# Two transformer layers on one core: the four norms worked in two parts of the tokens

## The chip, the cores and the metric

The kernel runs on one core of a Trainium2 chip. The metric is the device time of one execution in microseconds (us). TensorE (PE) multiplies, VectorE (DVE), ScalarE (ACT) and GpSimd (POOL) do the rest, SyncE (SP) issues the transfers.

## What is computed

```python
for i in range(DEPTH):                       # 2 layers, 1024 features
    sh1, sc1, g1, sh2, sc2, g2 = ada_modulation(c, ada_w[i], ada_b[i])
    a_lat = h * (1 + sc1) + sh1              # the same for 256 context tokens
    y = attn_mixer(...) if i % 2 == 0 else gla_mixer(...)
    h = layer_norm(DEEPNORM_ALPHA * h + g1 * y, ln_g[i, 0], ln_b[i, 0])
    f = conv_ffn(h * (1 + sc2) + sh2, ffn_w_up[i], ...)
    h = layer_norm(DEEPNORM_ALPHA * h + g2 * f, ln_g[i, 1], ln_b[i, 1])
```

The first layer works on 512 latent and 256 context tokens, 768 in all; behind its second norm the context is needed by the GLA mixer's states, and from there on only the 512 latent tokens have a residual stream. So there are four layer norms: norm 0 behind the attention projection and norm 1 behind the first FFN, over 768 tokens, norm 2 behind the GLA output and norm 3 behind the last FFN, over 512.

## The kernel before, in words

Features lie on the partitions, tokens in the free dimension. `h_res` holds the residual stream as 8 tiles (KT) of 128 features by 768 tokens. A weight matrix is cut into slabs: one slab is the weights of one output tile, 128 by 1024. There are 185 of them, in one fixed order over the whole kernel, read by SyncE into four `raw` buffers. ScalarE rounds a slab to fp32r (`w_hi`, L940), VectorE takes the rest (`w_lo`, L1358), both in two buffers. Activations are split alike into `x_hi` and `x_lo`. A slab is then 3 products per input tile: w_hi x_hi, w_hi x_lo, w_lo x_hi (`slab`, L464), each over 512 tokens and, where the context is in, over 256 more. FFN down slabs of the last group have 6 input tiles instead of 8.

Each engine runs its own hand-written list, and semaphores tie them. Around a norm the lists say:

- TensorE: the last eight slabs (numbers 0 to 7), then `stats`: products of `mean_w` with the sum of tiles 0 to 6 (L541), then with tile 7 and its square (L548), then two products per 128 tokens that spread mean and inverse root over the partitions (L531). Then `first_modulated`: the first two slabs of the next matrix together, tile by tile as x_hi and x_lo come (L505, L510); the second of them leaves out the last 2 tiles (3 over 512 tokens) until the first is done.
- ScalarE, per slab: w_hi of the slab after next, the gated copy out of PSUM (`tmp`, L1060, L1062), the square (`sq_t`, L1070). Then the root (L1087) and per tile `mod_t` (L959) and `x_hi` (L970).
- VectorE, per slab: w_lo, the residual (L1563), the running sum (L1570). In norm 0 it also makes modulation values of the next stages (L1382, L1384) behind slabs 1, 3 and 5, and `fuse` behind slab 6. Then five small operations (L1615 to L1626), the reciprocal (L1629), and over each tile of `h_res` two passes: less the mean (L1634), times the inverse root (L1640), both read from PSUM. x_lo of tiles 0, 3, 6 (L1646).
- GpSimd: the running sum of the squares (L1940), x_lo of the other five tiles (L1922).
- In norm 3 there is no modulation: ScalarE applies gain and bias (L1091) and SyncE writes each of the 8 tiles out (L445).

Everything runs over all tokens of the norm at once.

## Time and profile before

| | |
|---|---|
| median of 3 runs | 1747.23 us (1746.46 to 1747.8) |
| the profiled execution's own time | 1749.78 us |
| its span | 1748.0 us |
| mean granted TensorE clock | 0.985 |
| TensorE busy | 1671.9 us, 96% |
| TensorE weight loads | 1398.0 us, 80% |
| VectorE busy | 1122.3 us, 64% |
| ScalarE busy | 713.5 us, 41% |
| GpSimd busy | 85.9 us, 5% |

Busy time of TensorE counts matmuls with modelled ends, and they overlap: a mean matmul lasts longer than the distance to the next. The distance from start to start is what one costs in a stream. The granted clock is in shares of 2.4 GHz.

### The profile page before, as it was taken

Reading aid. Unit: us, or ns where it says so; the run is one execution under the profiler, and the core shown is the slowest. Engines: PE = TensorE matmul, PEld = TensorE weight load, DVE = VectorE, ACT = ScalarE, POOL = GpSimd, SP = SyncE. Lnnn points to the kernel's source line nnn. Section 1 sums busy time; section 2 is a strip of 40 time slices with the busy share of each in tenths; the row PEclk is TensorE's granted clock in tenths of the full one; section 3 lists DMA queues with packets and bytes.
Section 4 is the critical chain, followed back from the end, with each engine's and each line's share of the span. In section 5 each row is a group of like instructions: output and inputs, shape, how many; then the busy total and the mean of one; then the engine's idle time right before and its main releaser. Section 6 shows DMA issues by size and latency. Waiting matters only on the chain.

```text
span 1748.0 us, 23892 instructions
## 1 busy us (share of the span) xinstructions
PE 1671.9 (96%) x9008; PEld 1398.0 (80%) x9008; DVE 1122.3 (64%) x1816; ACT 713.5 (41%) x1060; POOL 85.9 (5%) x57
## 2 busy tenths in 40 slices
PE   7999999998999999999999899989989899999997
PEld 6888877887888888888888787857677688888885
DVE  6678666477787577864865554187755664464456
ACT  4212565335333223322334663256544543343345
POOL 0200000122000000000002200000002100000002
PEclk9999999999999999999999999999989999999998
DMA  8344100031433334333322112011112233333332
GB/s 355 110 149 157 49 1 1 25 133 39 143 122 121 130 108 144 104 136 133 109 62 85 49 49 61 24 35 37 37 49 84 62 96 95 96 96 97 96 96 73
DMA packets 37280, 159.51 MB, mean 91 GB/s; under 512 B 4145, under 2 KB 4401, under 8 KB 31057
## 3 DMA queue, kind: packets, MB, share of 16 engines
q1 hardware_dynamic: 37202, 158.44, 27.4%
q8 instruction: 52, 0.85, 0.2%
q14 instruction: 26, 0.21, 0.0%
HBM read 156.33 MB, written 2.10 MB: 91 GB/s over the span
## 4 chain that ended last, share of the span: by engine, by line
PE 87%; DVE 5%; ACT 4%; issue 2%; DMA 1%; SPq 0%; POOL 0%; ACTq 0%; DVEq 0%
PE pm L464 65%; PE pm L698 4%; PE pm L874 3%; PE pm L618 2%; PE pm L484 2%; PE pm L644 2%; PE pm L817 2%; PE pm L631 1%; ACT mod_t L959 1%; DMA ada_w<-first_ada 1%; PE pm L799 1%; DVE h_res L1634 1%; PE pm L575 1%; ACT w_hi L940 1%; PE pm L531 1%
## 5 line engine op out<-in xcount | busy, mean ns | idle before, releaser
L1358 DVE TENSOR_TENSOR w_lo<-raw,w_hi 128x1024 fp32r<-128x1024 f32 x185 | 230.4, 1247 | 374.2 <-ACT w_hi L940 371.7
L940 ACT ACTIVATE w_hi<-raw 128x1024 fp32r<-128x1024 f32 x181 | 191.8, 1060 | 638.3 <-PE pm L464 576.1
L464 PE MATMUL pm<-x_hi,w_hi 128*128 128x512 f32 (+1 forms) x1536 | 446.1, 352 | 3.6 <-DVE w_lo L1358 3.6
L464 PE MATMUL pm<-x_hi,w_lo 128*128 128x512 f32 (+1 forms) x1536 | 448.7, 354 | 0.0
L464 PE MATMUL pm<-x_lo,w_hi 128*128 128x512 f32 (+1 forms) x1536 | 444.1, 351 | 0.0
L464 PEld LDWEIGHTS pm<-x_hi,w_hi 128*128 128x128 f32 x1536 | 250.2, 189 | 49.4 <-DVE w_lo L1358 6.0
L464 PEld LDWEIGHTS pm<-x_hi,w_lo 128*128 128x128 f32 x1536 | 248.8, 189 | 39.6
L464 PEld LDWEIGHTS pm<-x_lo,w_hi 128*128 128x128 f32 x1536 | 247.2, 188 | 41.4
L464 PE MATMUL pm<-hid_hi,w_hi 128*128 128x512 f32 (+1 forms) x396 | 119.5, 356 | 1.7 <-DVE w_lo L1358 1.7
L464 PE MATMUL pm<-hid_hi,w_lo 128*128 128x512 f32 (+1 forms) x396 | 120.7, 359 | 0.0
L464 PE MATMUL pm<-hid_lo,w_hi 128*128 128x512 f32 (+1 forms) x396 | 119.3, 355 | 0.0
L1384 DVE CUSTOM_DVE_ANT_0 ada_w<-ada_w,cond_rep 128x1024 f32<-128x1024 f32 x80 | 102.5, 1281 | 0.0
L1940 POOL TENSOR_TENSOR sum<-sum,sq_t 128x768 f32<-128x768 f32 (+1 forms) x28 | 46.9, 1674 | 953.0 <-ACT sq_t L1070 953.0
L1126 ACT ACTIVATE hid_hi<-hid_f 128x768 f32 (+3 forms) x44 | 32.6, 741 | 124.6 <-DVE hid_f L1695 124.6
L464 PEld LDWEIGHTS pm<-hid_hi,w_hi 128*128 128x128 f32 x396 | 65.7, 189 | 14.9 <-DVE w_lo L1358 3.0
L464 PEld LDWEIGHTS pm<-hid_hi,w_lo 128*128 128x128 f32 x396 | 65.3, 188 | 10.8
L464 PEld LDWEIGHTS pm<-hid_lo,w_hi 128*128 128x128 f32 x396 | 64.7, 188 | 11.2
L874 PE MATMUL pm<-x_sum,raw 128*128 128x512 f32 x128 | 60.8, 610 | 8.4 <-issue 8.4
L1382 DVE CUSTOM_DVE_ANT_0 junk_f<-ada_w,cond_rep 128x1024 f32<-128x1024 f32 x56 | 68.3, 1219 | 0.0
L1698 DVE TENSOR_TENSOR hid_lo<-hid_f,hid_hi 128x512 f32 (+2 forms) x44 | 36.3, 825 | 44.7 <-ACT hid_hi L1126 44.7
L618 PE MATMUL pm<-qkv 128*128 128x256 f32 (+3 forms) x176 | 55.3, 419 | 2.1 <-ACT probs_t L1006 1.3
L644 PE MATMUL pm<-probs_t,v_tok 128*128 128x128 f32 x400 | 53.9, 279 | 1.5 <-DVE x_lo L1493 0.7
(224 smaller groups left out, 2363.2 us busy)
## 6 DMA issues: line engine op xcount, KB each, us to landing
raw<-slabs SPq DMA_DIRECT2D x185, 512.0 KB, 3.6
ada_w<-ada SPq DMA_DIRECT2D x44, 1024.0 KB, 4.9
ada_w<-first_ada SPq DMA_DIRECT2D x4, 1024.0 KB, 19.1
raw<-gates SPq DMA_DIRECT2D x8, 512.0 KB, 3.6
h_res<-x SPq DMA_DIRECT2D x4, 768.0 KB, 17.1
out<-h_res SPq DMA_DIRECT2D x8, 256.0 KB, 2.0
rope<-rope SPq DMA_DIRECT2D x1, 512.0 KB, 23.9
level_f<-level SPq DMA_DIRECT2D x1, 448.0 KB, 3.3
```

The source lines that it names most:

```text
L464: last = pe.matmul(out_p[:, a:b], w[slot][:, ks], x[:, k, a:b], start=(k == 0 and w is w_hi and x is hi), stop=(k == tiles - 1 and w is w_lo))
L484: last = pe.matmul(pm[slot][:, a:b], w[slot][:, ks], x[:, k, a:b], start=(n == 0 and w is w_hi and x is hi), stop=(n == KT - 1 and w is w_lo))
L618: last = pe.matmul(pm[n % 3][:, at:at + b - a], q, qkv[:, u["k"], a:b], start=True, stop=(u["band"] is None or at > 0))
L644: last = pe.matmul(weighed(n), v_tok[:, t, u["v"] * P:(u["v"] + 1) * P], probs_t[:, n % 2, j * P:(j + 1) * P], start=(j == 0), stop=(j == ...
L698: last = pe.matmul(pm[j][:, a:b], w[slot][:, ks], x[:, k, a:b], start=(k == 0 and w is w_hi and x is hid_hi), stop=(k == tiles - 1 and w i ...
L874: last = pe.matmul(gate_bank, gate_raw(i)[:, k * P:(k + 1) * P], x_sum[k][:, :], start=(k == 0), stop=(k == KT - 1))
L940: act.activation(w_hi[nxt % 2][:, :], raw[nxt % 4][:, :], ACT.Copy).then_inc(sem["split_hi"], 1)
L1358: dve.tensor_tensor(w_lo[nxt % 2][:, :], raw[nxt % 4][:, :], w_hi[nxt % 2][:, :].bitcast(FP32), ALU.subtract).then_inc(sem["split_lo"], 1)
L1382: junk_written = order.mark(dve.tensor_tensor_reduce(junk[:, :], w, cond_rep[:, 0, :], 1.0, 0.0, ALU.mult, ALU.add, to[:, half, 0:1]))
L1384: last = dve.tensor_tensor_reduce(w, w, cond_rep[:, 1, :], 1.0, 0.0, ALU.mult, ALU.add, to[:, half, 1:2])
L1698: dve.tensor_tensor(hid_lo[:, bass.ds(2 * i + u // 2, 1), 0:tokens].rearrange("p a b -> p (a b)"), hid_f[:, 0:tokens], hid_hi[:, bass.ds(2 ...
L1940: pool.tensor_tensor(sum2[:, 0:tokens], sum2[:, 0:tokens], sq_t[:, n % 2, 0:tokens], ALU.add).then_inc(sem["summed"], 1)
```

## The change

A norm is worked in two parts of its tokens (`norm_halves`): 0 to 511 and 512 to 767 where it has 768, 0 to 255 and 256 to 511 where it has 512. `h` is the part, `TAIL` is slab 6.

- TensorE's `tail` runs slab 6 and slab 7 over the first part, then the first part's sums (`first_sums`), slab 6 over the second part, the sums with tile 7 (`last_sums`), half of slab 7 over the second part, the spreading of the first part's statistics, the rest of slab 7, and the second part's sums. `first_modulated` goes through 16 places, the 8 tiles of the first part and then the 8 of the second; the second slab runs two places behind the first, and the second part's statistics are spread behind place 4. The third slab (`slab_high_first`) does all products with w_hi before those with w_lo.
- ScalarE and VectorE take slabs 6 and 7 out of PSUM part by part (`take`, `squares`, `half`), find mean and root part by part (`variance`, `root`, `inverse`), and interleave the second part's with the normalising of the first. All passes over `h_res`, `mod_t`, `x_hi`, `x_lo` are one part wide. Both slabs' splits for the next matrix now stand inside the tail and the first part.
- GpSimd's last sum and its x_lo are one part wide. SyncE writes 16 pieces instead of 8.
- In norm 0 VectorE's modulation values stand behind slabs 1, 2 and 4, `fuse` behind slab 5.

The diff, cut to its core:

```diff
-RESIDUALS = (KT, 4 * KT, 5 * KT, 8 * KT)
+RESIDUALS = (0, 3 * KT + 2, 4 * KT + 4, 7 * KT + 6)
+TAIL = KT - 2
+PER_NORM = KT + 2
...
+        def norm_halves(tokens):
+
+            return ((0, LAT), (LAT, TOK)) if tokens == TOK else ((0, CTX), (CTX, LAT))
...
+            def slab_high_first(base, u, hi, lo, tokens, banks):
...
+                for w, xs in ((w_hi, (hi, lo)), (w_lo, (hi,))):
+                    if w is w_lo:
+                        pe.wait_ge(sem["split_lo"], s + 1)
+                    for k in range(KT):
+                        for x in xs:
+                            for a, b in halves:
+                                last = pe.matmul(out_p[:, a:b], w[slot][:, k * P:(k + 1) * P], x[:, k, a:b],
+                                                 start=(k == 0 and w is w_hi and x is hi),
+                                                 stop=(k == KT - 1 and w is w_lo))
+                last.then_inc(sem["slab_done"], 1)
...
-                one, two = base % 2, (base + 1) % 2
-                for k in range(KT):
-                    slots = (one, two) if k < KT - lag else (one,)
-                    pe.wait_ge(sem["x_hi_done"], KT * (c + 1) + k + 1)
-                    for slot in slots:
-                        high(slot, k)
-                    pe.wait_ge(*low_of(c, k))
-                    for slot in slots:
-                        last = low(slot, k)
-                last.then_inc(sem["slab_done"], 1)
-                for k in range(KT - lag, KT):
-                    high(two, k)
-                    last = low(two, k)
-                last.then_inc(sem["slab_done"], 1)
...
+                def visit(j, i):
+                    if tokens == LAT and i == KT:
+                        low(j, *places[i - 1])
+                    if i < len(places):
+                        high(j, *places[i])
+                    if i >= 1 and not (tokens == LAT and i == KT):
+                        low(j, *places[i - 1])
+                behind = 2
+                pe.wait_ge(sem["split_lo"], base + 1)
+                for i in range(len(places) + behind + 1):
+                    if i < len(places):
+                        h, k = places[i]
+                        pe.wait_ge(sem["x_hi_done"], modded(c, h, k))
+                    if i <= len(places):
+                        visit(0, i)
+                    if i == behind:
+                        pe.wait_ge(sem["split_lo"], base + 2)
+                    if i >= behind:
+                        visit(1, i - behind)
+                    if i == 4:
+                        spread_stats(c, 1, tokens)
...
+                half_slab(TAIL, 0)
+                half_slab(TAIL + 1, 0)
+                first_sums(c, 0, tokens)
+                half_slab(TAIL, 1)
+                last_sums(c, 0, tokens)
+                half_slab(TAIL + 1, 1, 0, tiles // 2)
+                spread_stats(c, 0, tokens)
+                half_slab(TAIL + 1, 1, tiles // 2)
+                first_sums(c, 1, tokens)
+                last_sums(c, 1, tokens)
...
+                    take(TAIL, 0)
+                    squares(TAIL, 0)
+                    take(TAIL + 1, 0)
+                    squares(TAIL + 1, 0)
+                    take(TAIL, 1)
+                    if norm < 3:
+                        split(base + KT, base + KT)
+                    root(norm, 0, tokens)
+                    squares(TAIL, 1)
...
+                take, squares = last_half
+                for h, (a, b) in enumerate(norm_halves(tokens)):
                     for n in range(KT):
-                        act.wait_ge(sem["centred"], KT * c + n + 1)
-                        act.activation(h_res[:, n, 0:tokens], h_res[:, n, 0:tokens], ACT.Identity, bias=col("ln_b", KT * c + n),
-                                       scale=col("ln_g", KT * c + n)).then_inc(sem["h_ready"], 1)
-                    return
-                for n in range(KT):
-                    act.wait_ge(sem["centred"], KT * c + n + 1)
-                    modulate(n, c, tokens)
-
-            residual_phase(S_ATTN_OUT, 0, G1, TOK, norm=0)
-            norm_phase(0, TOK)
+                        act.wait_ge(sem["centred"], normed_at(c, h, n))
+                        if c < 3:
+                            modulate(n, c, h, tokens)
+                        else:
+                            act.activation(h_res[:, n, a:b], h_res[:, n, a:b], ACT.Identity, bias=col("ln_b", KT * c + n),
+                                           scale=col("ln_g", KT * c + n)).then_inc(sem["h_ready"], 1)
+                        if h == 0 and n == 0:
+                            take(KT - 1, 1)
+                            if c < 3:
+                                split(after_base + 1, after_base + 1)
+                            squares(KT - 1, 1)
+                        if h == 0 and n == 2:
+                            root(c, 1, tokens)
...
-                            if j in (1, 3, 5):
+                            if j in (1, 2, 4):
...
+                    half(TAIL, 0)
+                    half(TAIL + 1, 0)
+                    variance(norm, 0, tokens)
+                    half(TAIL, 1)
+                    inverse(norm, 0, tokens)
+                    if norm < 3:
+                        rest(base + KT, base + KT)
...
+                    dve.wait_ge(sem["spread"], 4 * c + 2 * h + 1)
+                    less_mean(0)
+                    dve.wait_ge(sem["spread"], 4 * c + 2 * h + 2)
+                    scaled(0)
+                    if h == 0:
+                        last_half(KT - 1, 1)
+                    for n in range(1, KT + 3 if c < 3 else KT + 1):
+                        if n < KT:
+                            less_mean(n)
+                        if 2 <= n <= KT:
+                            scaled(n - 1)
+                        if h == 0 and n == 2 and c < 3:
+                            rest(after_base + 1, after_base + 1)
+                        if h == 0 and n == 4:
+                            variance(c, 1, tokens)
+                        if h == 0 and n == 6:
+                            inverse(c, 1, tokens)
...
+            for h, (a, b) in enumerate(norm_halves(LAT)):
+                for n in range(KT):
+                    sp.wait_ge(sem["h_ready"], KT * h + n + 1)
+                    sp.dma_start(out[:, n, a:b], h_res[:, n, a:b]).then_inc(sem["out_done"], 16)
...
+                for h, (a, b) in enumerate(norm_halves(tokens)):
+                    pool.wait_ge(sem["squared_h"], PER_NORM * c + TAIL + 1 + 2 * h)
+                    pool.wait_ge(sem["summed"], KT * c + TAIL + h)
+                    pool.tensor_tensor(sum2[:, a:b], sum2[:, a:b], sq_t[:, TAIL % 2, a:b], ALU.add).then_inc(sem["summed"], 1)
```

The order of VectorE's instructions in norm 0, before, from the last residual on. L1563 is the residual of slab 7, L1358 w_lo of the next slab, L1634 the subtraction of the mean, L1640 the scaling:

```order
L1607 TENSOR_TENSOR fused<-fused,mods 128x16
L1563 SCALAR_TENSOR_TENSOR h_res<-h_res,tmp 128x768
L1358 TENSOR_TENSOR w_lo_61<-raw_55,w_hi_59 128x1024
L1615 COPY stat_a<-pm 128x12
L1619 TENSOR_TENSOR small<-pm,stat_a 128x6
L1621 TENSOR_TENSOR small<-small 128x6
L1623 TENSOR_TENSOR small<-stat_a,small 128x6
L1626 TENSOR_TENSOR small<-pm,small 128x6
L1629 RECIPROCAL small<-small 128x6
L1634 TENSOR_TENSOR h_res<-h_res,pm 128x768 x3
L1640 TENSOR_TENSOR h_res<-h_res,pm 128x768
L1634 TENSOR_TENSOR h_res<-h_res,pm 128x768
```

And in the change, from the residual half of slab 6 over the second part (L1720) to the first part's third tile. L1790 is the reciprocal, L1488 w_lo, L1797 the subtraction, L1802 the scaling:

```order
L1720 SCALAR_TENSOR_TENSOR h_res<-h_res,tmp 128x256
L1726 TENSOR_TENSOR sum_96<-sum_96,h_res 128x256
L1790 RECIPROCAL small<-small 128x4
L1488 TENSOR_TENSOR w_lo_60<-raw_54,w_hi_58 128x1024
L1797 TENSOR_TENSOR h_res<-h_res,pm 128x512
L1802 TENSOR_TENSOR h_res<-h_res,pm 128x512
L1720 SCALAR_TENSOR_TENSOR h_res<-h_res,tmp 128x256
L1797 TENSOR_TENSOR h_res<-h_res,pm 128x512 x2
L1802 TENSOR_TENSOR h_res<-h_res,pm 128x512
L1488 TENSOR_TENSOR w_lo_61<-raw_55,w_hi_59 128x1024
L1797 TENSOR_TENSOR h_res<-h_res,pm 128x512
L1802 TENSOR_TENSOR h_res<-h_res,pm 128x512
```

The last residual half and two splits now stand between reciprocal and third tile, and the passes are 512 wide in the first part.

ScalarE's in norm 0, before, around the root (L1087):

```order
L1060 ACTIVATE tmp<-pm,mods 128x512
L1060 ACTIVATE tmp<-pm,mods 128x256
L1070 ACTIVATE sq_t<-h_res 128x768
L940 ACTIVATE w_hi_59<-raw_55 128x1024
L1087 ACT_TABLE_LOAD
L1087 ACTIVATE small<-small,vec 128x6
L959 ACTIVATE x_hi<-h_res,fused 128x512
L959 ACTIVATE x_hi<-h_res,fused 128x256
L959 ACTIVATE mod_t<-h_res,fused 128x512
L959 ACTIVATE mod_t<-h_res,fused 128x256
L959 ACTIVATE mod_t<-h_res,fused 128x512
```

And in the change. L1175 is the copy out of PSUM, L1014 the split of a slab, L1186 the square, L1209 the root, L1046 the modulation, L1056 x_hi:

```order
L1175 ACTIVATE tmp<-pm,mods 128x256
L1014 ACTIVATE w_hi_58<-raw_54 128x1024
L1209 ACT_TABLE_LOAD
L1209 ACTIVATE small<-small,vec 128x4
L1186 ACTIVATE sq_t<-h_res 128x256
L1046 ACTIVATE x_hi<-h_res,fused 128x512
L1046 ACTIVATE mod_t<-h_res,fused 128x512
L1175 ACTIVATE tmp<-pm,mods 128x256
L1014 ACTIVATE w_hi_59<-raw_55 128x1024
L1186 ACTIVATE sq_t<-h_res 128x256
L1046 ACTIVATE mod_t<-h_res,fused 128x512
L1056 ACTIVATE x_hi<-mod_t 128x512
```

A copy, a split and a square stand between the modulations of tile 0 and tile 1. The rows that follow there, tile 2, the second part's root and tile 3:

```order
L1046 ACTIVATE mod_t<-h_res,fused 128x512
L1056 ACTIVATE x_hi<-mod_t 128x512
L1209 ACTIVATE small<-small,vec 128x2
L1046 ACTIVATE mod_t<-h_res,fused 128x512
L1056 ACTIVATE x_hi<-mod_t 128x512
```

Tile 3's modulation is behind the root in the list.

## Rows read from the trace of the kernel before

**Rows 1.** The page, part 1: busy us, share, instructions.
```profile
PE 1671.9 (96%) x9008; PEld 1398.0 (80%) x9008; DVE 1122.3 (64%) x1816; ACT 713.5 (41%) x1060; POOL 85.9 (5%) x57
```

**Rows 2.** Windows of A to D: span, busy by engine (records), PE clock, DMA share, GB/s.
```profile
387.06:421.73 34.67, 28.66 (x170) 23.78 (x169) 21.18 (x29) 23.66 (x34) 9.87 (x6) 0.95 0.05 16
964.57:998.79 34.22, 28.74 (x170) 24.04 (x168) 21.58 (x30) 23.22 (x33) 9.21 (x5) 0.95 0.05 16
1352.20:1377.85 25.65, 20.15 (x97) 15.22 (x97) 15.88 (x29) 15.81 (x23) 6.89 (x6) 0.93 0.07 24
1730.16:1748.00 17.84, 5.76 (x49) 5.40 (x48) 11.34 (x23) 9.18 (x12) 0.00 (x0) 0.73 0.31 118
```

**Rows 3.** Timeline in A: start us, us, engine, line, operation, [idle before].
```profile
387.06 2.84 PE L541 MATMUL pm<-mean_w,sum 128*128 128x128 f32 x24
...
391.27 1.28 ACT L1087 ACT_TABLE_LOAD   x1
...
394.49 2.68 DVE L1634 TENSOR_TENSOR h_res<-h_res,pm 128x768 f32<-128x768 f32 x3 [0.54 <-PE pm L531]
...
398.07 1.30 ACT L959 ACTIVATE x_hi<-h_res,fused 128x512 fp32r<-128x512 f32 x2 [4.35 <-DVE h_res L1640]
...
419.36 1.06 ACT L940 ACTIVATE w_hi<-raw 128x1024 fp32r<-128x1024 f32 x1 [2.59 <-PE pm L510]
```

**Rows 4.** Timeline, TensorE's products: in A over 768 tokens, in C over 512.
```profile
386.35 0.51 PE L464 MATMUL pm<-x_lo,w_hi 128*128 128x512 f32 x2
386.70 0.53 PE L464 MATMUL pm<-x_hi,w_lo 128*128 128x512 f32 x2
...
1351.78 0.39 PE L464 MATMUL pm<-o_lo,w_hi 128*128 128x512 f32 x1
1352.01 0.39 PE L464 MATMUL pm<-o_hi,w_lo 128*128 128x512 f32 x1
```

**Rows 5.** Timeline of ScalarE in A and C; last, a group by line and form.
```profile
405.50 1.29 ACT L959 ACTIVATE mod_t<-h_res,fused 128x512 f32<-128x512 f32 x2
...
407.57 1.30 ACT L959 ACTIVATE mod_t<-h_res,fused 128x512 f32<-128x512 f32 x2
...
1370.70 0.80 ACT L959 ACTIVATE mod_t<-h_res,fused 128x512 f32<-128x512 f32 x1
...
1371.53 0.63 ACT L970 ACTIVATE x_hi<-mod_t 128x512 fp32r<-128x512 f32 x1
...
1372.07 0.80 ACT L959 ACTIVATE mod_t<-h_res,fused 128x512 f32<-128x512 f32 x1
...
L959 ACT ACTIVATE mod_t<-h_res,fused 128x256 f32<-128x256 f32 x16 | 9.4, 586 | 0.0
```

**Rows 6.** Timeline in D: VectorE's last passes and ScalarE's last step.
```profile
1742.01 0.68 DVE L1634 TENSOR_TENSOR h_res<-h_res,pm 128x512 f32<-128x512 f32 x1
...
1742.60 1.87 DVE L1640 TENSOR_TENSOR h_res<-h_res,pm 128x512 f32<-128x512 f32 x3
1743.32 2.22 ACT L1091 ACTIVATE h_res<-h_res,vec 128x512 f32<-128x512 f32 x3 [0.38 <-DVE h_res L1640]
```

**Rows 7.** Timeline of VectorE in the GLA heads: passes of 256 columns.
```profile
1153.15 0.42 DVE L1773 TENSOR_TENSOR sides<-cum 128x256 f32<-128x256 f32 x1
1153.48 0.42 DVE L1774 TENSOR_TENSOR sides<-cum 128x256 f32<-128x256 f32 x1
```

**Rows 8.** Timeline of GpSimd: x_lo over 768 tokens and over 512.
```profile
412.69 1.84 POOL L1922 TENSOR_TENSOR x_lo<-mod_t,x_hi 128x768 fp32r<-128x768 f32 x1 [1.01 <-ACT x_hi L970]
...
1368.81 1.29 POOL L1922 TENSOR_TENSOR x_lo<-mod_t,x_hi 128x512 fp32r<-128x512 f32 x1 [1.45 <-ACT x_hi L970]
```

**Rows 9.** Windows of low clock in A and C; timeline, TensorE's first product in C.
```profile
400.70:404.00 3.30, 3.21 (x11) 2.42 (x10) 3.30 (x4) 2.51 (x4) 1.28 (x1) 0.52 0.00 0
...
1364.20:1366.60 2.40, 2.40 (x7) 1.83 (x7) 2.40 (x5) 2.07 (x3) 1.55 (x2) 0.53 0.00 0
...
1361.92 0.47 PE L505 MATMUL pm<-x_hi,w_hi 128*128 128x512 f32 x1 [2.38 <-ACT x_hi L959]
```

330 lines of the change are left out of this document (200 added, 130 removed).

## The prediction

> **What bounds the kernel now.** I read the page first: TensorE is busy 1671.9 of 1748.0 us [rows 1], so what a change can win lies where TensorE stands still or does small work, or behind its last product. The stretches around the four norms, taken next, hold this [rows 2]. A is the norm behind the attention projection (from the last product of its last slab to the first of the third FFN slab, 34.67 us), B the norm ahead of the GLA projections (to the first logits, 34.22 us), C the norm behind the GLA output (25.65 us), D the last norm (17.84 us, to the end of the span).
>
> How much of A is idle TensorE? A slab over 768 tokens has 24 pairs of a 512-wide and a 256-wide product, one pair each 0.352 us [rows 4], so 8.45 us, and the two slabs inside A are 16.9. The 36 statistics products are about 8.2 (12 of them take 2.84 with the tail of the last [rows 3]). So 9.6 us are idle in A, 9.1 in B. In C a slab over 512 tokens is 24 x 0.228 = 5.5 us [rows 4], two are 10.9, 24 statistics products 5.5: 9.2 idle. D has no slabs after it. 28 us is thus the most that A to C could give.
>
> What makes it wait is a chain of short steps: sums, root, spread, the subtraction of the mean at 394.49, x_hi of tile 0 from 398.07 [rows 3], and then one tile per ScalarE period, 2.07 us over 768 tokens (405.50 to 407.57) and 1.37 over 512 (1370.70 to 1372.07) [rows 5]. Two slabs want 2.11 and 1.37 us of TensorE per tile, so it is paced by ScalarE there. D is VectorE's: 16 passes over h_res, started 0.60 us apart (1742.01, 1742.60), then ScalarE's last step and the last transfer [rows 6].
>
> **Prices of the narrow pieces.** One 256-wide product is 0.352 - 0.228 = 0.125 us, so two halves cost 0.250 where one 512-wide product cost 0.228. Over 768 tokens the cut at 512 is where it was, and TensorE's work stays; over 512 tokens C has 4 slabs x 24 products x 0.022 = 2.1 us more, D 2 x 18 x 0.022 = 0.8. On VectorE 512 columns start 0.60 us apart [rows 6], 256 columns 0.335 (1153.15 to 1153.48) [rows 7]: 0.07 more for each pass cut in two. The 256-column rows read no PSUM, the norm's passes do; I take the same price. In the Trainium skill, "VectorE: DVE Perf Modes", section on the TRN2 errata, an fp32 tensor_tensor takes (N + 151) / 0.96 ns, which is 0.42 for 256, and small tiles pay the fixed part each. The durations here agree (0.42), the starts do not: half of the fixed part lies under the next pass. By the page the passes of D would take 32 x 0.42 - 16 x 0.69 = 2.4 us longer.
>
> By the rows they take 1.1 longer, and the sum goes by the rows. On ScalarE the modulation of 256 columns takes 0.586, the copy 0.42 (0.63 for 512 less half of what 1024 columns take more [rows 5, 3]), with a hand-off of 0.03 and 0.09 under the next: 0.94 a tile, over 512 columns 1.37. A tile of A or B therefore costs 2.31 where it cost 2.07, one of C 1.88 where it cost 1.37: 1.9 and 4.1 us more over eight tiles, on the engine that paces. GpSimd's 1.84 and 1.29 [rows 8] give 0.75 for 256 columns, within ScalarE's period.
>
> **Stage A, step by step**, on the clock of the profiled run. Slab 6 starts at 387.06 - 16.9 = 370.2. Its first part ends at 375.6, that of slab 7 at 381.1 (24 x 0.228 each). VectorE, which meets the last block of modulation products now behind slab 4 and not behind slab 5, comes out of its fuse near 377.4 by my list, so residual, square and GpSimd's sum of slab 6, first part, are there at 380.2: in time. first_sums to 382.9, slab 6 second part (24 x 0.125) to 385.9, last_sums to 387.7. ScalarE, behind take(6,1), the split of the next slab (1.06) and a table load of 1.28 [rows 3], has the root at 389.2; reciprocal 389.5, w_lo 390.7, and the first mean subtraction at 390.8, against 394.49: 3.7 us earlier. Scale at 391.5, x_hi of tile 0 out near 393.1 (was 399.4). Then four new things stand in the way. On ScalarE: mod, take(7,1), split (1.06), square, to 395.6. On VectorE: the residual half, then a w_lo between tiles 2 and 3. TensorE waits for the second part's last_sums until 396.1, then for tiles 1 and 2 (398.0, 400.4). And ScalarE's second Sqrt stands ahead of tile 3 (shown with the change) and waits for VectorE's variance, which comes only behind tiles 3 and 4: 400.4 to 402.0. So x_hi of tile 3 is ready at 403.4 (for all 768 tokens it was by 407.57 [rows 5]). From there TensorE has 14.6 us of products and 0.9 of spreads left and, with ScalarE at 1.37 a tile (it wants 1.37 itself), has no reason to stop: slab 0 done 418.1, slab 1 at 418.9. The third slab now needs only w_hi: 418.1 + 0.1 + 1.06 = 419.3, where it began at 421.73. **A: 2.4 us won**, if the clock holds. It does not now: in A the granted clock is 0.52 from 400.7 to 404.0 (the level of 1.2 GHz), in C 0.53 from 1364.2 to 1366.6, there behind an idle stretch of 2.38 us [rows 9]. After the change TensorE does some 2.3 us of products between 396 and 403.4, in bursts; I expect the same fall, from about 401.5, of which 2 us lie in dense work and cost 1.0. **A: 1.4 won.**
>
> **Stage B** has six tiles in slabs 6 and 7, so less work to lie under the statistics: slab 6 starts at 964.57 - 12.7 = 951.8, first parts end at 955.9 and 960.0, the root is ready at 967.4, w_lo at 968.9, first subtraction at 968.9. By the distances of A slab 0 ends at 968.9 + 27.3 = 996.2, slab 1 at 997.0. The logits wait for w_hi and then take_low on ScalarE, to 998.2 (was 998.79 [rows 2]): 0.5 won, less 1.0 for the clock. **B: 0.5 lost.**
>
> **Stage C.** Slab 6 starts at 1341.3; the narrow halves end at 1344.3 and 1347.3, GpSimd's sum lets first_sums go at 1347.6, the root is ready at 1353.5, VectorE starts at 1355.1. ScalarE then does 8 x 0.94 for each part with the square, split and Sqrt in between: x_hi of the last tile 1375.5, GpSimd's x_lo 1376.2, slab 0 done 1376.4, third slab 1377.6 (was 1377.85 [rows 2]). A low clock is hidden by ScalarE's pace. **C: 0.2 won**, call it nothing.
>
> **Stage D.** Slab 6 starts at 1722.0; TensorE waits 0.3 for w_lo, and 1.4 ahead of first_sums, because square, residual and GpSimd's 0.75 of slab 6 come behind those of slab 5. The root is ready at 1733.5, subtraction starts at 1734.1. From there VectorE has 32 passes x 0.335 = 10.7, the last residual half 0.45 and 1.2 of waiting for it (ScalarE takes slab 7's second part only at 1735.8), five small statistics and a reciprocal inside the first part, 1.2: its end is 1747.8, where it was 1744.5 [rows 6]. The narrow last ScalarE step and transfer give back 0.3. **D: 3.0 lost.** Output goes out in 16 transfers for 8; fifteen lie under the passes.
>
> Sum: -1.4 + 0.5 + 0 + 3.0 = +2.1 us. The profiled execution took 1749.78 for a span of 1748.0, the median of the runs is 1747.23; on the median the forecast is **1749.3 us**, on the profiled span 1750.1. Bounds by rows: A from 0.9 lost (low clock all through the first part) to 4 won (no wait for the second Sqrt), B 2.8 lost to 2.1 won, C 1.2 lost to 1.3 won, D 1 to 4 lost.
>
> **Rivals.** (1) *As worked out*, 0.38, with 1747 to 1752 of its own. (2) *The chain is shorter than I make it*: the variance of the second part does not hold ScalarE up (1.6 us), and TensorE's gaps stay short enough for 2.4 GHz. Then A 3.9, B 2.1, C 1.3 won, D 2.6 lost: 1742.5. For it: 28 us of idle are there, and the small steps overlap better in a real queue than in my list. Against it: the clock falls in A and C now, in C behind only 2.4 us. 0.27. (3) *No fall of the clock, all else as in 1*: 2.4 + 0.5 + 0.2 - 3.0 = 0.1 won, 1747.1. This is also where the change does not do what it says and only trades one wait for another. 0.15. (4) *Slower*: the bursts of two or three products between waits keep TensorE at 1.2 GHz well into the dense part. With twice the low stretch that A has now, 6.6 us at half speed in dense work cost 3.3 in A and B, and 1.4 in C: A 0.9, B 2.8, C 1.2, D 3.0 lost, 1755.1. It decides once more than 3 us of dense work run low. For it: the rows of the clock [rows 9], and TensorE is now the pacing engine from tile 3 on, so nothing hides it. Against: the quiet stretch is no longer than now. 0.20.
>
> The Trainium skill, "TensorE: Matmul & The Clock Gate", section on HAM oscillation, describes this: bursts with waits between them let the gate fall back each time. The fall behind 2.4 us of idle in C agrees.
>
> **Numbers.** 0.2%, 3.5 us, is about what a measurement can tell here: faster is below 1743.7, slower above 1750.7. Case 2 is faster in three of four; case 4 is slower nearly always, case 1 in one of four. That gives faster 0.24, same 0.46, slower 0.30. The range of 1742 to 1755 leaves out the ends of cases 2 and 4.
>
> **What would show it.** First subtraction of the mean 3 to 4 us nearer to slab 6's start in A, B and C; ScalarE idle ahead of the second Sqrt by 1 to 2 us; TensorE without waits from tile 3 on; a low granted clock between tile 1 and tile 5; D longer by 3 us with VectorE back to back at 0.335. I am wrong if a 256-wide product follows another at more than 0.13 us, if first_sums waits for GpSimd in A or B, or if D does not grow.

## The result, and the profile after

| | before | after |
|---|---|---|
| median of 6 runs each | 1746.65 us (1744.91 to 1747.8) | 1755.68 us (1753.95 to 1758.62) |
| the profiled execution's own time | 1749.78 us | 1758.62 us |
| its span | 1748.0 us | 1756.8 us |
| mean granted TensorE clock | 0.985 | 0.981 |

The ratio is 1.0053, 95% interval 1.004 to 1.0066: slower, clear of its interval, and just above the forecast's range. The page of after, part 1 (columns as in [rows 1]):

```profile
PE 1678.8 (96%) x9140; PEld 1409.5 (80%) x9140; DVE 1138.0 (65%) x1925; ACT 726.3 (41%) x1114; POOL 92.0 (5%) x76
```

Against [rows 1] every engine is busier, TensorE by 6.9 us, VectorE by 15.7, ScalarE by 12.8. To see where the span grew I cut both traces at the same places of the program: A from the attention output's first product to the third FFN slab, FFN 0 with its down slabs (504.30 us before, 504.31 after, not shown), B from just ahead of its last six down slabs to the logits, G from there to the GLA output's first product, C from that to the third slab of FFN 1, F to FFN 1's last six down slabs, D from those to the end. (These stretches are longer than the prediction's of the same letters, and each holds the same norm.) Windows of the kernel before (us of the window, TensorE's busy us and records, granted clock, DMA share, GB/s):

```profile
315.62:421.73 106.11, 98.61 (x573) 0.98 0.21 70
926.03:998.79 72.76, 67.28 (x388) 0.98 0.20 60
998.79:1299.20 300.41, 279.02 (x1473) 0.96 0.15 46
1299.20:1377.85 78.65, 68.97 (x315) 0.96 0.18 54
1377.85:1704.64 326.79, 324.60 (x1428) 1.00 0.32 97
1704.64:1748.00 43.36, 30.80 (x158) 0.89 0.21 73
```

The same windows of the kernel after:

```profile
314.92:418.58 103.66, 97.02 (x573) 0.98 0.21 72
922.89:997.42 74.53, 67.71 (x388) 0.95 0.19 59
997.42:1301.06 303.64, 282.20 (x1472) 0.95 0.14 45
1301.06:1382.24 81.18, 72.10 (x411) 0.94 0.17 52
1382.24:1708.66 326.42, 324.51 (x1428) 1.00 0.31 97
1708.66:1756.80 48.14, 34.53 (x194) 0.86 0.20 66
```

So A won 2.45 us, B lost 1.77, G 3.23, C 2.53, D 4.78; F and what lies ahead of A gave 0.4 and 0.7 (that first stretch, which no version touches, took 311.35 to 315.62 us in the fourteen traces behind this document, so its 0.7 is scatter). The sum is the 8.8 us between the spans. G is surprising: nothing in it but the order of one slab's products was changed. What differs is the clock's column. Stretches at the lower level (1.2 GHz) stand out in narrower windows of after:

```profile
398.40:402.40 4.00, 2.93 (x6) 0.57 0.21 83
975.20:983.20 8.00, 6.95 (x17) 0.57 0.09 35
999.20:1006.40 7.20, 7.20 (x21) 0.53 0.45 142
1364.80:1372.00 7.20, 5.87 (x29) 0.53 0.12 51
1732.80:1737.60 4.80, 4.69 (x27) 0.64 0.00 0
```

and of before:

```profile
400.00:404.00 4.00, 3.91 (x14) 0.57 0.00 0
976.80:980.80 4.00, 3.86 (x13) 0.57 0.00 0
1362.40:1366.40 4.00, 3.75 (x10) 0.58 0.00 0
999.20:1006.40 7.20, 7.20 (x35) 1.00 0.47 148
1722.00:1734.00 12.00, 12.00 (x72) 1.00 0.00 0
```

With 1 minus the clock, times two, times the width, after has 6.9 us at the lower level in B where before has 3.4, 6.8 behind the logits where before has none, 6.8 in C where before has 3.4, and 3.5 in D ahead of the last sums where before has none.

G's 3.2 us are almost wholly the fall behind the logits. ScalarE's third copy of the keys out of PSUM, before and then after, with the logits at 998.79 and 997.42:

```profile
1019.48 0.79 ACT L1144 ACTIVATE gla_k<-pm 128x768 f32<-128x768 f32 x1
```

```profile
1021.25 0.79 ACT L1276 ACTIVATE gla_k<-pm 128x768 f32<-128x768 f32 x1
```

That is 20.69 us behind the logits before and 23.83 after, 3.14 more, and from there to the GLA output only 0.09 more are lost.

One thing has to be known for reading the experiments: two of their traces show FFN 0 in 494.8 and 494.9 us and not in 504.3, and the kernel before spread from 1731.84 to 1750.95 us on their chips, so the ratios are good to some 0.3% only, and I rest the verdicts on the stages of the traces.

### The profile page after: what moved, and what is told of

It is laid out like the page before. It is cut to its first block, busy times and chain, and to the rows that moved or that the text cites. A ratio compares the mean times of both kernels' runs of the same rounds, so it can differ in the third digit from the quotient of the medians.

```text
span 1756.8 us, 24419 instructions
## 1 busy us (share of the span) xinstructions
PE 1678.8 (96%) x9140; PEld 1409.5 (80%) x9140; DVE 1138.0 (65%) x1925; ACT 726.3 (41%) x1114; POOL 92.0 (5%) x76
## 4 chain that ended last, share of the span: by engine, by line
PE 85%; DVE 8%; ACT 3%; issue 2%; DMA 1%; SPq 0%; POOL 0%; ACTq 0%; DVEq 0%
PE pm L500 58%; PE pm L782 4%; PE pm L961 3%; PE pm L703 2%; PE pm L536 2%; PE pm L520 2%; PE pm L729 2%; PE pm L904 2%; PE pm L482 1%; DVE w_lo L1488 1%; PE pm L716 1%; DMA ada_w<-first_ada 1%; PE pm L625 1%; PE pm L886 1%; ACT w_hi L1027 1%
## 5 line engine op out<-in xcount | busy, mean ns | idle before, releaser
L1488 DVE TENSOR_TENSOR w_lo<-raw,w_hi 128x1024 fp32r<-128x1024 f32 x185 | 231.2, 1251 | 353.0 <-ACT w_hi L1027 349.5
L500 PE MATMUL pm<-x_hi,w_hi 128*128 128x512 f32 (+1 forms) x1464 | 429.9, 355 | 2.9 <-DVE w_lo L1488 2.9
L500 PE MATMUL pm<-x_hi,w_lo 128*128 128x512 f32 (+1 forms) x1464 | 424.8, 351 | 0.0
L500 PE MATMUL pm<-x_lo,w_hi 128*128 128x512 f32 (+1 forms) x1464 | 424.3, 351 | 0.0
L500 PEld LDWEIGHTS pm<-x_hi,w_hi 128*128 128x128 f32 x1464 | 237.5, 189 | 42.4 <-DVE w_lo L1488 4.2
L500 PEld LDWEIGHTS pm<-x_lo,w_hi 128*128 128x128 f32 x1464 | 238.4, 189 | 41.1
L500 PEld LDWEIGHTS pm<-x_hi,w_lo 128*128 128x128 f32 x1464 | 236.1, 189 | 39.5
L500 PE MATMUL pm<-hid_hi,w_hi 128*128 128x512 f32 x360 | 110.0, 360 | 1.4 <-DVE w_lo L1488 1.4
L500 PE MATMUL pm<-hid_hi,w_lo 128*128 128x512 f32 x360 | 108.3, 355 | 0.0
L500 PE MATMUL pm<-hid_lo,w_hi 128*128 128x512 f32 x360 | 108.3, 355 | 0.0
L500 PEld LDWEIGHTS pm<-hid_hi,w_hi 128*128 128x128 f32 x360 | 59.3, 188 | 12.3 <-DVE w_lo L1488 2.6
```

The lines of the kernel that those rows point to most:

```text
L500: last = pe.matmul(out_p[:, a:b], w[slot][:, ks], x[:, k, a:b], start=(k == 0 and w is w_hi and x is hi), stop=(k == tiles - 1 and w is w_lo))
L1488: dve.tensor_tensor(w_lo[nxt % 2][:, :], raw[nxt % 4][:, :], w_hi[nxt % 2][:, :].bitcast(FP32), ALU.subtract).then_inc(sem["split_lo"], 1)
```

## The experiments

There are three groups of four kernels (e1 to e4, e5 to e8, e9 to e12). Each group ran on one chip of its own, with runs of the kernel before, whose medians were 1746.37, 1738.47 and 1741.57 us. Theory C says that the clock took most of the 8.8 us. Theory W says that the new waits and narrow pieces themselves did. Rival P says that low stretches come and go with the place of the program in time. In us, per stage:

| | A | B | G | C | F | D |
|---|---|---|---|---|---|---|
| before | 106.11 | 72.76 | 300.41 | 78.65 | 326.79 | 43.36 |
| change | 103.66 | 74.53 | 303.64 | 81.18 | 326.42 | 48.14 |
| e1_busy | 103.68 | 73.04 | 296.22 | 80.09 | 326.40 | 46.72 |
| e2_first_norm_only | 103.49 | 73.07 | 299.64 | 80.21 | 326.47 | 43.26 |
| e3_last_norm_whole | 105.08 | 73.02 | 301.62 | 81.10 | 326.39 | 43.32 |
| e4_cut_at_384 | 105.30 | 75.54 | 301.21 | 84.54 | 326.40 | 48.02 |
| e5_change_again | 103.64 | 74.42 | 305.46 | 82.61 | 326.53 | 48.25 |
| e6_before_busy | 106.11 | 72.73 | 302.24 | 80.16 | 326.72 | 43.30 |
| e7_first_norm_busy | 103.68 | 72.36 | 298.89 | 78.66 | 326.53 | 43.30 |
| e8_later_second_root | 103.42 | 72.93 | 303.42 | 80.28 | 326.44 | 48.92 |
| e9_narrow_passes_alone | 105.32 | 72.01 | 301.35 | 78.67 | 326.79 | 44.06 |
| e10_busy_at_logits_alone | 103.70 | 73.01 | 301.56 | 81.06 | 326.46 | 48.24 |
| e11_first_sums_later | 104.36 | 73.27 | 303.54 | 81.31 | 326.45 | 44.35 |
| e12_candidate | 103.39 | 73.11 | 300.67 | 80.16 | 326.49 | 43.27 |

The same traces by their low clock: us at the lower level in the first slabs of norms 0, 1 and 2, in the 10 us behind the logits, and in D ahead of the last sums. The last column is the place of that third copy of the keys, in us behind the logits.

| | A | B | logits | C | D | keys |
|---|---|---|---|---|---|---|
| before | 3.4 | 3.4 | 0 | 3.4 | 0 | 20.69 |
| change | 3.4 | 6.8 | 6.8 | 6.8 | 3.4 | 23.83 |
| e1_busy | 0 | 0 | 0 | 0 | 0 | 20.69 |
| e2_first_norm_only | 3.4 | 6.8 | 3.4 | 3.4 | 0 | 22.26 |
| e3_last_norm_whole | 3.4 | 6.8 | 3.4 | 6.8 | 0 | 22.53 |
| e4_cut_at_384 | 6.8 | 13.6 | 3.4 | 10.2 | 0 | 22.53 |
| e5_change_again | 3.4 | 6.8 | 6.8 | 6.8 | 3.4 | 24.09 |
| e6_before_busy | 0 | 0 | 0 | 0 | 0 | 21.00 |
| e7_first_norm_busy | 0 | 0 | 0 | 0 | 0 | 21.00 |
| e8_later_second_root | 0 | 0 | 6.8 | 6.8 | 3.4 | 23.84 |
| e9_narrow_passes_alone | 6.8 | 3.4 | 3.4 | 3.4 | 0 | 22.53 |
| e10_busy_at_logits_alone | 3.4 | 6.8 | 3.4 | 6.8 | 3.4 | 22.53 |
| e11_first_sums_later | 3.4 | 3.4 | 3.4 | 6.8 | 0 | 22.25 |
| e12_candidate | 0 | 0 | 0 | 0 | 0 | 20.99 |

**e1_busy.** TensorE does small products on constants into a free PSUM bank ahead of its waits.

```diff
+            def keep_busy(count, bank=2):
+                for _ in range(count):
+                    pe.matmul(pm[bank][:, 0:P], mean_w[:, 0:1].to_broadcast([P, P]), eye[:, :], start=True, stop=True)
...
+                        keep_busy({1: (5, 5, 1), 2: (0, 0, 1), 3: (8, 8, 6), 4: (0, 0, 0, 0)}.get(i, (0, 0, 0))[c])
                         pe.wait_ge(sem["x_hi_done"], modded(c, h, k))
...
+                keep_busy((3, 6, 3, 0)[c])
                 last_sums(c, 1, tokens)
```

> The changed kernel, with TensorE kept busy in its waits: spread-like matmuls on constants into a PSUM bank that nobody reads, placed ahead of the waits for the first sums, the last sums, tiles 1 and 3 of the norms' first slabs and the logits (1.0 to 2 us of them for a wait of 0.6 to 2 us). Theory C (the clock): of the 8.9 us between the kernels, about 7 are granted clock that falls for 6.8 us instead of 3.4 in norms 1 and 2, for 6.8 us behind the logits and for 3.4 us in norm 3. Then these stretches go (and so do the 3.4 us that norms 0 to 2 had in the kernel before): 1744 to 1748 us, ratio to before 0.999 to 1.001, mean clock up from 0.981 to 0.99 or more. Theory W (the waits themselves: GpSimd's sum, the second root, narrow passes on VectorE): nothing is gained, 1755 to 1758 us, whatever the clock does.

Measured: 1748.5 us median, ratio 1.0033 [1.0009, 1.0057], just above what Theory C was given, clock 0.991. The windows of its trace:

```profile
315.14:418.82 103.68, 100.61 (x615) 1.00 0.21 72
923.13:996.17 73.04, 71.74 (x448) 1.00 0.20 60
996.17:1292.39 296.22, 273.17 (x1474) 0.98 0.15 46
1292.39:1372.48 80.09, 74.02 (x445) 0.98 0.18 53
...
1698.88:1745.60 46.72, 34.62 (x208) 0.88 0.21 68
```

No step was moved by this edit, yet the span falls by 11.2 us against the change's first trace: B by 1.49, G by 7.42, C by 1.09, D by 1.42, A not at all. Of G's 7.42 us, 3.2 lie behind the logits, where the fall is gone. The others are not the change's: G is 4.2 us shorter than in the kernel before, through low stretches deeper in the GLA heads (some 24 us low in G before, 31 in the change, 10 here) where nothing was filled. So the clock took 1.5 + 3.2 + 1.1 + 1.4 = 7.2 of the 8.8 us, which is Theory C's side. But the norms do not come back to before: at the full clock B is still 0.3 over, C 1.4, D 3.4. Both theories hold a part.

**e2_first_norm_only.** The names `SPLIT` and `parts_of` were added so that each norm can be whole or in two parts; counts of the semaphores follow.

```diff
+SPLIT = (1, 0, 0, 0)
```

> Only norm 0 in two parts, norms 1, 2 and 3 as in the kernel before. Both theories: norm 0 gains the 1.9 us that its stretch showed. Theory C: no other stretch changes, as each low stretch comes from what stands right before it: 1744.5 to 1745.5 us, ratio 0.9990. Rival P (the low clock comes and goes with the phase of the program, so any shift of time can add stretches elsewhere): 1746 to 1750 us, with low stretches behind the logits or in norm 2 as in the changed kernel.

1744.65 us, 1.0011 [0.9986, 1.0036]. A is 2.6 us shorter, more than expected; B had 6.8 us of low clock from 971.3 on and is only 0.3 longer; C's 1.6 more lie ahead of its first product (64.28 us for 62.72), where the clock fell a second time among the GLA output's slabs; from there on it takes 15.93 as before. The ratio could not show the 2 us. A low stretch of 3.4 us stood behind the logits here too, so the fall there is not the divided norm 1's alone: Rival P is right on that.

**e3_last_norm_whole.** `SPLIT = (1, 1, 1, 0)`.

> The change with norm 3 left whole, norms 0 to 2 in two parts. If the 4.8 us of the last stretch are all the split's (3.0 for the narrow passes, 1.8 for GpSimd's sum, the low clock and the late start): 1750.8 us, ratio 1.0025. If what is over the 3.0 comes from elsewhere: 1752.7 us or more, ratio 1.0035.

1750.64 us, 1.0035 [1.001, 1.0061]. The median lies where the first of the two readings has it. D is 43.32: all 4.8 us of the last stretch are the division's. Its A is worth a look too, for here the clock fell later:

```profile
393.20:401.60 8.40, 3.86 (x15) 1.00 0.23 64
401.60:405.60 4.00, 4.00 (x13) 0.57 0.00 0
405.60:418.54 12.94, 12.63 (x84) 1.00 0.00 0
```

against the change's own:

```profile
394.82:398.40 3.58, 1.45 (x7) 1.00 0.30 58
398.40:402.40 4.00, 2.93 (x6) 0.57 0.21 83
402.40:418.58 16.18, 15.62 (x94) 1.00 0.00 0
```

Both begin with the first product of the norm's first slabs. The same 3.4 us of low clock cost nothing when they ended 7.5 us behind it (23.76 us in all; 23.77 in e1_busy with none), and 1.6 when they ended 12.1 behind it (25.34): TensorE is fed by ScalarE up to tile 3 and bounds the stage from there. B says the same: 24.5 to 24.6 us from its first product with no low clock (e1_busy, e8) or with 6.8 us that ended 7.4 us behind it (e3, e10), 26.0 to 26.1 where the low clock ended 11.0 to 12.6 behind it (change, e5, e11).

**e4_cut_at_384.**

```diff
-            return ((0, LAT), (LAT, TOK)) if tokens == TOK else ((0, CTX), (CTX, LAT))
+            return ((0, LAT), (LAT, TOK)) if tokens == TOK else ((0, 3 * P), (3 * P, LAT))
```

> The change with the cut of norms 2 and 3 at token 384 instead of 256. Theory W: norm 3's second part is half as wide, so behind the second root each pass is shorter and the last stretch loses 0.5 to 1.5 us less; norm 2 about the same: 1754 to 1755.3 us. Theory C: first tiles of norm 2 come further apart (1.4 us instead of 0.95) while each gives TensorE more columns, the clock still falls for 6.8 us: 1754 to 1757 us.

1757.71 us, 1.0091 [1.0055, 1.0127]. D lost 4.7 again, though no low stretch stood ahead of its sums, B 2.8, with the code of the change and 13.6 us at the lower level, and C 5.9, with 10.2. Theory W's gain in D did not come, for the trace has VectorE's passes over 384 columns start 0.46 us apart and those over 128 columns 0.20: the two together take what two of 256 do (0.33 each), and from the first subtraction to the end D takes 16.62 us as in the change. C's price was not taken apart further here.

**e5_change_again.** The changed kernel, unaltered.

> The changed kernel once more, unaltered. If the low clock of its first trace belongs to the code (Theory C in its strict form), the same stretches are low again, each for the same time, and the stages come out within 0.2 us: 1754 to 1757 us. If the fall is a matter of where the engine's gaps happen to lie (Rival P), stretches move, appear or go, and a stage's length follows its own low time: up to 3 us between two traces of one stage, median 1751 to 1757.

1757.62 us, 1.0107 [1.0075, 1.0139]. A, B and D came back within 0.15 us with the same low stretches; behind the logits 6.8 us again. G and C were 1.8 and 1.4 longer, C with one more low stretch among the GLA output's slabs (62.21 us to its first product, 60.77 in the change's first trace). So that the clock falls in these norms belongs to the code, and G scatters by 2 us between executions of one kernel. Where and how long it falls does not belong to the code alone, and here Rival P holds a part: norm 1 is the same code in e3, e4 and e10, and its first low stretch began 4.4 us behind the first product in the change, 4.2 in e5, 0.6 in e3, 0.5 in e10 and 0.4 us ahead of it in e4; B took 74.53, 74.42, 73.02, 73.01 and 75.54 us.

**e6_before_busy.** `SPLIT = (0, 0, 0, 0)`, and TensorE kept busy in the whole norms.

```diff
+                    if not SPLIT[c] and j == 2 and c < 3:
+                        keep_busy(2, 0, TOK)
...
+                    if k == 0:
+                        keep_busy((14, 14, 9)[c], 0, TOK)
                     pe.wait_ge(sem["x_hi_done"], modded(c, 0, k))
```

> The kernel before, with TensorE kept busy ahead of the spread of the root and of the first tile in norms 0 to 2 (3.5, 3.5 and 2.3 us of idling there). The three low stretches of 3.4 us in the norms go. Where TensorE bounds these stages this gives up to 1.7 us each, 5 in all; ScalarE paces norm 0's and norm 1's first tiles, so 1.5 to 3 us less than the kernel before: ratio 0.9983 to 0.9991. Against the changed kernel kept busy this gives the price of the division with the clock taken out: by the stages of e1_busy norm 0 wins 2.4, norm 1 loses 0.3, norm 2 loses 1.4, norm 3 loses 3.4, so e1_busy is 2.7 us slower than this kernel.

1737.17 us, 0.9993 [0.9965, 1.002], A and B at 106.11 and 72.73 as in the kernel before: a miss. The low stretches of the norms were gone and nothing was won: in a whole norm ScalarE paces the first slabs, and it hid them. In C the part from the first product was 16.01 us, 15.93 before; its 1.5 us more lie ahead of that, with one more fall among the output's slabs.

**e7_first_norm_busy.** `SPLIT = (1, 0, 0, 0)` with both kinds of busy work.

> Norm 0 alone in two parts, and TensorE kept busy in the waits of norms 0 to 2. Both gains add up if they are independent: 2.4 us below e6_before_busy, ratio to before 0.997 to 0.998. If the busy work in norm 0 costs what it gains (its products delay the first tiles): as e6_before_busy.

1744.76 us, 1.0034 [1.0012, 1.0055]: by the ratio a miss, as e6's median lies lower (8 of its 12 runs below 1738.3 us). By the trace A has its 2.4 us and no norm lost (B took 72.36 us, with the quicker pace of products that FFN 0 shows). Its profiled run was 1733.72 us, with FFN 0 at 494.95.

**e8_later_second_root.**

```diff
-                        if h == 0 and n == 2:
+                        if h == 0 and n == 4:
                             root(c, 1, tokens)
...
-                        if h == 0 and n == 6:
+                        if h == 0 and n == KT:
                             inverse(c, 1, tokens)
```

> The change with ScalarE's second root behind tile 4 instead of tile 2 of the first part, and VectorE's reciprocal behind its last tile. Theory W2 (ScalarE bounds norm 2, and its idle 1.3 to 1.8 us ahead of the second root stand in the path): norm 2's stretch from the first product to the third slab falls by 1.2 us (20.4 to 19.2), norms 0 and 1 by 0 to 1: 1753 to 1755 us if the clock leaves it alone. Rival: the roots' spread comes so late that TensorE and with it the second part wait for it: norm 2 no shorter or longer, 1756 us or more.

1750.19 us, 1.0065 [1.0045, 1.0085]. ScalarE in C from the first product to the third slab, by form; of the change:

```profile
L1046 ACT ACTIVATE mod_t<-h_res,fused 128x256 f32<-128x256 f32 x15 | 8.8, 590 | 1.0 <-DVE h_res L1802 1.0
L1056 ACT ACTIVATE x_hi<-mod_t 128x256 fp32r<-128x256 f32 x14 | 5.9, 419 | 0.4
...
L1209 ACT ACTIVATE small<-small,vec 128x2 f32<-128x2 f32 x1 | 0.3, 296 | 1.3 <-DVE small L1783 1.3
```

and of e8:

```profile
L1046 ACT ACTIVATE mod_t<-h_res,fused 128x256 f32<-128x256 f32 x15 | 8.8, 591 | 1.9 <-DVE h_res L1802 1.9
...
L1209 ACT ACTIVATE small<-small,vec 128x2 f32<-128x2 f32 x1 | 0.3, 279 | 0.0
```

The 1.3 us of idling ahead of the root went, and this part of C fell from 20.41 to 19.59 us with the same 6.8 us of low clock: 0.8 for 1.2 expected, as ScalarE now waits 0.9 longer for VectorE's scaling. A stayed (23.75), so there the wait was covered, and D lost 0.8 more, where VectorE paces and the second part had to wait 1.00 us for the spread of the late root. What was not expected is the clock: it did not fall in A or B, and B took 72.93 us for 74.53. TensorE's wait ahead of tile 3 was 0.85 and 0.84 us there (2.06 and 2.05 in e11, where the clock was full ahead of it and the root stands at its old place). One trace shows this.

**e9_narrow_passes_alone.** `SPLIT = (0, 0, 0, 0)`, and in norm 3 only the passes in halves.

```diff
+                    for h, (a, b) in enumerate(norm_halves(LAT)):
+                        for n in range(KT + 2):
+                            if n < KT:
+                                dve.tensor_tensor(h_res[:, n, a:b], h_res[:, n, a:b], pm[3][:, a:b],
+                                                  ALU.subtract).then_inc(sem["less_mean"], 1)
```

> The kernel before, with one thing of the change: the last norm's passes, ScalarE's last step and the output transfers go in two halves of 256 tokens, behind statistics taken over all 512. If the starts 0.335 us apart are the whole price of narrow passes, VectorE needs 32 x 0.335 = 10.7 us for 16 x 0.60 = 9.6, and the narrower last steps give 0.3 to 0.6 back: from the first sums to the end 18.4 to 18.7 us (17.8 whole, 23.9 in the change). If narrow passes cost their full 0.42 us each, 21 us. The rest of the change's 4.8 us is then the second statistics and the waits.

From the first sums to the end 18.57 us for 17.84: 0.73 us, as the starts 0.335 us apart would have it. 1738.18 us, 0.9994 [0.9968, 1.0021]; in this trace FFN 0 took 494.80 us, and its A and B are 0.8 shorter with the same quicker pace of products.

**e10_busy_at_logits_alone.**

```diff
                 if j == 0:
+                    keep_busy(5, 3)
                     pe.wait_ge(sem["low_done"], 1)
```

> The changed kernel with five extra small matmuls ahead of the wait for the logits, and nowhere else. The idle 1.0 us there is filled. Theory C: the low stretch of 6.8 us behind the logits goes or shrinks to 3.4 us, and the stretch from the logits to the GLA output's first slab falls from 303.6 to 305.5 us (its two traces) to 300.5 to 302; norms 1, 2 and 3 keep their low stretches and lengths. Rival: the fall behind the logits comes from the logits themselves (32 rows of 128 in use), which stay: nothing changes.

1753.65 us, 1.0071 [1.004, 1.0102]. G was 301.56 us with 3.4 us low behind the logits, inside the range expected for Theory C. C and D kept low stretches and lengths; B's fall came earlier and cost nothing. But this cannot be put down to the filled wait: e3 and e4 have the 1.04 us of idling ahead of the logits, as the change has, and show the same 3.4 us there, the keys at the same 22.53 and G at 301.62 and 301.21. Nor is that idling needed, as e2 and e9 have none and fell for 3.4 us too. What the logits' fall needs is not shown. The four traces in which TensorE was kept busy through norm 1 (e1, e6, e7, e12) have none; three of these have no busy work at the logits.

**e11_first_sums_later.**

```diff
                 half_slab(TAIL + 1, 0)
-                first_sums(c, 0, tokens)
                 half_slab(TAIL, 1)
+                first_sums(c, 0, tokens)
                 last_sums(c, 0, tokens)
```

> The change with one step of TensorE's order exchanged in all four norms: the first part's sums stand behind slab 6's second part instead of ahead of it, so that its products fill the wait for GpSimd's sum (0.44, 0.65, 1.11 and 1.97 us in norms 0 to 3). If this wait is in the path, the mean is spread earlier by it: norm 3 gains 1.5 to 2 us (dn1 to the end 48.1 to 46.4), norm 2 up to 1.1, norms 0 and 1 up to 0.6. If the last residual on VectorE (1.25 us beside GpSimd) bounds it too, norm 3 gains under 0.5.

1750.07 us, 1.0046 [1.0026, 1.0067], 5.6 us below the change's 1755.68 and 7.6 below e5's 1757.62, each on a chip of its own. D is 44.35: 3.8 us of its 4.8 came back with one line moved, twice what was expected. TensorE's timeline in D, products left out (start, us, engine, line, operation, idle before); of the change:

```profile
1732.91 1.52 PE L589 MATMUL pm<-mean_w,sum 128*128 128x128 f32 x8 [1.97 <-POOL sum L2123]
...
1737.57 0.61 PE L601 MATMUL pm<-mean_w,h_res 128*128 128x128 f32 x4
```

and of e11:

```profile
1730.98 1.11 PE L589 MATMUL pm<-mean_w,sum 128*128 128x128 f32 x8
1731.93 0.61 PE L601 MATMUL pm<-mean_w,h_res 128*128 128x128 f32 x4
```

Not only is the wait of 1.97 us gone. The change's wait brought the low clock on (it fell in the four traces with a wait of 1.95 to 1.97 us there, the change, e5, e8 and e10, and in none with less), and the products between first and last sums then ran at half speed; in e11 no stretch ahead of D's sums is low. C looks unchanged (81.31 for 81.18), but holds the second fall among the output's slabs that e5 had: against e5 its first product comes 1.3 us earlier (60.92 for 62.21), about the 1.11 us of waiting. A shows 0.9 us earlier tiles (78.98 for 79.90), eaten by a fall that ended 12.4 us behind the first product. B's tiles came 1.2 us earlier, and it took 73.27 for 74.53, with a fall of 3.4 us late in it.

**e12_candidate.** e7 with the first sums later.

> Norm 0 alone in two parts with its first sums behind slab 6's second part, norms 1 to 3 whole, TensorE kept busy ahead of the tiles of norms 0 to 2. Norm 0 from the attention output's first slab to the third FFN slab: 103.2 to 103.7 us against 106.1 before, the other norms as before, fewer low stretches: 2.5 to 4 us below the kernel before where FFN 0 takes the same time in both. If FFN 0's pace, which in one trace (e7_first_norm_busy) was 494.9 us for 504.3, is found with this kernel as seldom as in the earlier divided ones (about 3 of 25 runs, against 25 of 57 of the kernel before on the same chips), its median can still come out above that of before.

1744.15 us, 1.0012 [0.9992, 1.0033]; A 103.39 us, B 0.35 over before, D as before, clock 0.989, FFN 0 504.31 in the trace. C's 1.5 us more lie ahead of its first product (64.13 us), with the second fall among the output's slabs, as in e2 and e6. Its stages give 2.7 us on A, and all twelve runs lie between 1741.36 and 1748.16, while half of before's lie below 1742.5. So no version measured faster than the kernel before by more than its interval; that norm 0 in two parts shortens its own stage is shown by every trace, by 0.8 to 2.7 us, and by 2.4 or more wherever the clock did not fall late in it.

## Why the prediction was wrong

The forecast was 1749.3 us, the result 1755.68. The number came out at rival 4's 1755.1, but by luck: rival 4 has 0.9 us lost in A where 2.45 were won, 1.2 lost in C where 2.5 were, and nothing behind the logits where 3.2 were lost. Point by point, each stage at the full clock (e1_busy) and as it ran:

| | forecast | at full clock | as it ran |
|---|---|---|---|
| A | 1.4 won | 2.4 won | 2.45 won |
| B | 0.5 lost | 0.3 lost | 1.8 lost |
| behind the logits | nothing | nothing | 3.2 lost |
| C | nothing | 1.4 lost | 2.5 lost |
| D | 3.0 lost | 3.4 lost | 4.8 lost |

**The step that failed is the clock's.** I gave it one fall per norm as long as before's [rows 9], 1.0 us each in A and B, and hid it in C "by ScalarE's pace"; behind the logits and in D I gave it nothing. It fell twice as long in B and C, and also behind the logits and in D. B's term of 1.0 was 1.5. C's of 0 was 1.1, not by the slabs' products but because the products and the spreading of the second part's statistics came late: ScalarE idled 1.42 us for the second part's first tile (0.41 in e1_busy). D's of 0 was 1.4, the logits' of 0 was 3.2. A's of 1.0 was 0, as the fall ended before the dense part; it was 1.6 in e3 and e11, where it came later. In all the clock took 7.2 us for the 2.0 of the sum, 5.2 of the 6.7 us by which the sum missed the traces' 8.8; the rest is B and C below and 0.4 in D, less the 1.1 that F and the start gave. Rival 4 named the mechanism and the rows for it; I held against it that the quiet stretch is no longer than now, and the change divides a quiet stretch into several short ones. How much of the 3.2 us is the division's is less sure than the rest: the kernels with norm 1 whole and no busy work fell for 0 (before), 3.4 (e2) and 3.4 us (e9) behind the logits, those with it in two parts for 3.4 to 6.8. The Trainium skill, "TensorE: Matmul & The Clock Gate", section "HAM oscillation — how this bites in real kernels", speaks of bursts whose waits let the clock fall again each time. The traces agree for B, with 1.33, 1.17 and 0.96 us of waiting between its first products, and e1_busy, which fills them, shows no fall. But e8 has 1.33, 1.17 and 0.84 us there and does not fall, so these waits alone do not decide it.

**Stage A** otherwise went as worked out: 2.4 at full clock. The first subtraction came at 389.65, 20.7 us behind slab 6's start, where it was 24.3 before: 3.6 us nearer, 3.7 forecast. ScalarE was idle 1.80 us ahead of the second root and TensorE had no wait from tile 3 on, as named.

**Stage B** at full clock lost 0.3 where 0.5 was to be won: first_sums waited 0.65 us for GpSimd, which I had said would prove me wrong, and the logits waited 1.04 us for ScalarE's take_low. (Both waits are the change's own; e1_busy fills them without ending them sooner.)

**Stage C**: "0.2 won" was 1.4 lost without the clock. The sizes of a narrow tile were right (590 and 419 ns for 586 and 420), but I let ScalarE run without a stop but for the root. It waits for VectorE 0.29 and 0.75 us at tiles 1 and 2 and 1.26 ahead of the root in e1_busy. Moving the root gave 0.8 of it back (e8).

**Stage D**: behind the first subtraction the change takes 3.4 us more (16.62 for 13.18), where I had 3.7; the passes alone are 0.73 of it (e9), with what the narrower last steps give back, so the price by starts held and not the 2.4 us by durations. The start was the error: 0.7 us earlier by my list, 1.3 later in the trace (31.52 us into the stage for 30.18; 30.06 in e1_busy), through 1.97 us of waiting for 1.4 and the low clock behind it. With the sums later it starts at 27.89 (e11). What I did not see is that this wait needed only two neighbouring steps exchanged.

**The narrow pieces** were priced rightly throughout: products 0.12 us, VectorE's passes 0.33, a ScalarE tile 0.945 (forecast 0.125, 0.335 and 0.94).

## What to carry to other kernels

Dividing a serial stretch to overlap it makes many short waits out of a long one, and here the waits were paid a second time, in low clock: 7.2 of 8.8 us. Price the clock's fall not in the stage alone but in the dense work behind it, and in the step after that. Small products on constants ahead of the waits took the falls away (e1_busy), and gave nothing where another engine sets the pace (e6_before_busy). Keep products at hand for every wait: an independent block of work placed ahead of a sum that another engine still makes gave 3.8 us of 4.8 here. And divide only where the piece that paces keeps its width: norm 0, whose tokens were already worked as 512 and 256, won 2.4 us; norm 1, cut alike, came out even at the full clock; norms 2 and 3, whose 512 became twice 256, lost.
